# Cross-attention units of two heads and half the tokens, and three reordered steps, in a two-layer decoder trunk

## The reference, cut to what matters

```
for layer in 0, 1:
    h = RMSNorm(x);  p = h @ W_in                        # 768 columns for the mixer, 256 for the memory queries
    mix = mLSTM(p)            (layer 0, 4 heads of 192)
          DiffAttention(p)    (layer 1, 6 heads of 128)
    # memory cross-attention, 4 heads of 64, into 256 memory tokens
    q = RMSNorm(xq); k = RMSNorm(kv[:256]); v = kv[256:]
    s = q k^T / 8            per head: 512 x 256
    xo = softmax(s) v        per head: 512 x 64
    x = x + concat(mix, xo) @ W_out
    x = x + SwiGLU(RMSNorm(x))
```

## Time and profile before

| | |
|---|---|
| median of 3 runs | 1282.05 us (1280.47 to 1282.13) |
| the profiled execution | 1281.97 us |
| its span, first to last instruction | 1280.1 us, mean granted clock 0.997 |
| PE busy | 1259.7 us (98%) |
| POOL busy | 857.0 us (67%) |
| DVE busy | 538.2 us (42%) |
| ACT busy | 334.2 us (26%) |

### The profile page before, as it was taken

How to read it: one execution, slowest core, us unless ns; L and a number is a source line. 1 busy time by engine, 2 the same in 40 slices (tenths; PEclk the granted TensorE clock), 3 DMA queues, 4 the chain that set the end, 5 groups by cost and what they waited for, 6 DMA issues and landing times.

```text
span 1280.1 us, 15882 instructions
## 1 busy us (share of the span) xinstructions
PE 1259.7 (98%) x5762; PEld 1005.5 (79%) x5762; DVE 538.2 (42%) x798; ACT 334.2 (26%) x663; POOL 857.0 (67%) x1032
## 2 busy tenths in 40 slices
PE   7999999989999999999999999999999999999999
PEld 6888777668888888888878777777788888888887
DVE  6954334555333232213264777774733213321321
ACT  6423344622220011101122455553322001100110
POOL 7897332268777777777786444454677777777775
PEclk9999999999999999999999999999999999999999
DMA  7233111013222222322233222221222222232223
GB/s 258 95 129 116 50 34 50 33 54 103 98 99 99 99 86 96 99 98 99 78 119 115 66 67 66 62 75 61 74 92 98 99 98 97 90 98 94 98 78 103
DMA packets 34482, 115.92 MB, mean 91 GB/s; under 512 B 4349, under 2 KB 4862, under 8 KB 34302
## 3 DMA queue, kind: packets, MB, share of 16 engines
q1 hardware_dynamic: 32688, 111.16, 25.9%
q10 hardware_dynamic: 1742, 4.10, 1.2%
HBM read 110.00 MB, written 2.10 MB: 88 GB/s over the span
## 4 chain that ended last, share of the span: by engine, by line
PE 93%; DVE 3%; POOL 1%; issue 1%; ACT 1%; ACTq 0%; DMA 0%; SPq 0%; POOLq 0%
PE PS L1490 91%; POOL w_lo L543 1%; PE PS L1878 1%; DVE nmB L1397 1%; DVE acc L1028 1%; DVE xT L1286 0%; ACT tmp L596 0%; ACTq L847 0%; PE PS L1726 0%; DMA w_raw<-in_wt_dram 0%; PE PS L1904 0%; DVE PS L1395 0%; POOL w_hi L538 0%; PE PS L1689 0%; DVE tmp L1249 0%
## 5 line engine op out<-in xcount | busy, mean ns | idle before, releaser
L543 POOL TENSOR_TENSOR w_lo<-w_raw,w_hi 128x256 fp32r<-128x256 f32 x804 | 631.5, 816 | 17.1
L538 POOL TENSOR_SCALAR w_hi<-w_raw 128x1024 fp32r<-128x1024 f32 (+2 forms) x205 | 214.4, 1046 | 392.3 <-PE PS L1490 391.6
L1490 PE MATMUL PS<-Hh,w_hi 128*128 128x512 f32 x1072 | 432.2, 403 | 9.3 <-POOL w_lo L519 6.8
L1490 PE MATMUL PS<-Hh,w_lo 128*128 128x512 f32 x1072 | 419.0, 391 | 0.0
L1490 PE MATMUL PS<-Hl,w_hi 128*128 128x512 f32 x1072 | 418.7, 391 | 0.0
L1490 PEld LDWEIGHTS PS<-Hh,w_hi 128*128 128x128 f32 x1072 | 201.8, 188 | 67.1 <-issue 26.9
L1490 PEld LDWEIGHTS PS<-Hh,w_lo 128*128 128x128 f32 x1072 | 201.7, 188 | 43.0
L1490 PEld LDWEIGHTS PS<-Hl,w_hi 128*128 128x128 f32 x1072 | 202.1, 189 | 38.1 <-issue 1.0
L1490 PE MATMUL PS<-Ah,w_hi 128*128 128x512 f32 (+1 forms) x544 | 209.5, 385 | 0.8 <-POOL w_lo L543 0.7
L1490 PE MATMUL PS<-Al,w_hi 128*128 128x512 f32 (+1 forms) x544 | 205.4, 378 | 0.0
L1490 PE MATMUL PS<-Ah,w_lo 128*128 128x512 f32 (+1 forms) x544 | 205.3, 377 | 0.0
(11 more groups left out here) (247 smaller groups left out, 1000.6 us busy)
## 6 DMA issues: line engine op xcount, KB each, us to landing
w_raw<-in_wt_dram SPq DMA_DIRECT2D x181, 512.0 KB, 3.2
w_raw<-in_wt_dram SPq DMA_DIRECT2D x16, 384.0 KB, 3.0
w_raw<-in_wt_dram SPq DMA_DIRECT2D x8, 448.0 KB, 3.1
QKR<-QKP ACTq DMA_DIRECT2D x24, 128.0 KB, 4.3
xT<-in_x_t_dram SPq DMA_DIRECT2D x8, 256.0 KB, 5.8
out_dram<-xT SPq DMA_DIRECT2D x8, 256.0 KB, 2.0
mT<-in_mem_t_dram SPq DMA_DIRECT2D x1, 1024.0 KB, 9.2
cn<-in_constants_dram ACTq DMA_DIRECT2D x1, 580.5 KB, 6.0
```

Source lines behind the costliest of these rows:

```text
L538: nc.gpsimd.tensor_scalar(w_hi[:, sl, 0:nk], w_raw[:, raw, 0:nk], 0.0, 1.0, ALU.add, ALU.mult).then_inc(w_round, 1)
L543: lo = nc.gpsimd.tensor_tensor(w_lo[:, sl, w], w_raw[:, raw, w], w_hi[:, sl, w].bitcast(F32), ALU.subtract)
L1490: return nc.tensor.matmul(out_, a, b, start=start, stop=stop)
```

## The change

Four things.
1. In both layers a unit x now is **both heads of a pair (x // 2) and half the tokens (x % 2)**. The scores of a token tile are two adjacent products, head 0 on rows 0 to 63 and head 1 on rows 64 to 127, to different banks; the value product is, for each half of the memory tokens, two adjacent products with 64-column weights, head 0 to PSUM partitions 0 to 63 and head 1 to 64 to 127, of 256 moving columns each. The indices of scales and the tiles of `m_hi`, `m_lo` (now 128 x 256 instead of 64 x 512) follow. `c_pv` waits once, ahead of its loop.
2. Head 0: PE waits for 24 projection tiles, not 26; on ACT `cross_std(0)` comes before `head_num(0)`.
3. Last head, DVE: `m_p(3)` comes before `fill_out(7)` and `head_out(3)`.
4. Layer 0's output tile 0 is closed before tile 2 is opened, then tile 2 is opened, then 1 and 2 are closed.

```
 m_s(x), c_s(x):
-                r = 64 * (x % 2)
-                for t in range(NT):
-                    last = mm(PS[:, M_BANK[t // 2], (t % 2) * MEM:(t % 2 + 1) * MEM], xqA[r:r + 64, x // 2, t * P:(t + 1) * P],
-                              xk[r:r + 64, 0, x // 2])
-                    if t % 2:
-                        last.then_inc(ms_done, 1)
+                for i in range(2):
+                    t = 2 * (x % 2) + i
+                    for hd in range(2):
+                        r = 64 * hd
+                        last = mm(PS[:, M_BANK[hd], i * MEM:(i + 1) * MEM], xqA[r:r + 64, x // 2, t * P:(t + 1) * P],
+                                  xk[r:r + 64, 0, x // 2])
+                        if i:
+                            last.then_inc(ms_done, 1)
 m_pv(x), c_pv(x):
-                    last = mm(PS[r:r + 64, M_BANK[0]], xv[:, 0, mt, x * 64:(x + 1) * 64], M_PT[mt], start=mt == 0, stop=mt == 1)
+                    for hd in range(2):
+                        h = 2 * (x // 2) + hd
+                        last = mm(PS[64 * hd:64 * hd + 64, M_BANK[0], 0:MEM], xv[:, 0, mt, h * 64:(h + 1) * 64],
+                                  M_PT[mt][:, hd * MEM:(hd + 1) * MEM], start=mt == 0, stop=mt == 1)
 m_hi(x), and likewise m_lo, c_hi, c_lo:
-                nc.scalar.activation(Ah[r:r + 64, MC + x // 2], PS[r:r + 64, M_BANK[0]], ACT.Copy).then_inc(mo_hi, 1)
+                nc.scalar.activation(Ah[:, MC + x // 2, q], PS[:, M_BANK[0], 0:MEM], ACT.Copy).then_inc(mo_hi, 1)
 ACT, heads:
+                if h == 0:
+                    cross_std(0)
                 head_num(h)
                 if h == 0:
                     v_out(4)
-                    cross_std(0)
 DVE, heads:
                 m_max(h)
                 if h == MH - 1:
+                    m_p(h)
                     fill_out(2 * h + 1)
                 head_out(h)
...
-            m_p(MH - 1)
             mixer_out(DONE_MC, MC)
 PE, head_scores(0):
-                    pe.wait_ge(dense_free, T_HEAD)
+                    pe.wait_ge(dense_free, T_HEAD - 2)
 PE, output tiles of layer 0:
             out_blocks(1, (0, 1, 2, 3, 6), after=lambda i: m_pv(MH - 1) if i == 2 else None)
+            out_blocks(0, (4, 5, 7))
             out_blocks(2, (0, 1, 2, 3, 6))
-            for j in range(3):
-                out_blocks(j, (4, 5, 7))
+            out_blocks(1, (4, 5, 7))
+            out_blocks(2, (4, 5, 7))
```

More of the change, by code:

```diff
@@ L768, in m_exp @@
                     j = 4 * x + t
-                    nc.scalar.activation(M_P[t], PS[:, M_BANK[t // 2], (t % 2) * MEM:(t % 2 + 1) * MEM], ACT.Exp,
-                                         scale=rqA[:, x // 2, t, x % 2:x % 2 + 1], bias=nmA[:, j:j + 1],
+                    hd, q = t // 2, 2 * (x % 2) + t % 2
+                    nc.scalar.activation(M_P[t], PS[:, M_BANK[hd], (t % 2) * MEM:(t % 2 + 1) * MEM], ACT.Exp,
+                                         scale=rqA[:, x // 2, q, hd:hd + 1], bias=nmA[:, j:j + 1],
                                          accum_out=rsA[:, j:j + 1]).then_inc(ms_exp, 1)
@@ L780, in m_hi @@
             def m_hi(x):
-                r = 64 * (x % 2)
+                q = slice(MEM * (x % 2), MEM * (x % 2 + 1))
                 act.wait_ge(mo_done, x + 1)
-                nc.scalar.activation(Ah[r:r + 64, MC + x // 2], PS[r:r + 64, M_BANK[0]], ACT.Copy).then_inc(mo_hi, 1)
+                nc.scalar.activation(Ah[:, MC + x // 2, q], PS[:, M_BANK[0], 0:MEM], ACT.Copy).then_inc(mo_hi, 1)
             cross_sq(0, 0)
@@ L915, in c_exp @@
                     j = 4 * x + t
-                    nc.scalar.activation(C_P[t], PS[:, C_BANK[t // 2], (t % 2) * MEM:(t % 2 + 1) * MEM], ACT.Exp,
-                                         scale=rqB[:, x // 2, t, x % 2:x % 2 + 1], bias=nmX[:, j:j + 1],
+                    hd, q = t // 2, 2 * (x % 2) + t % 2
+                    nc.scalar.activation(C_P[t], PS[:, C_BANK[hd], (t % 2) * MEM:(t % 2 + 1) * MEM], ACT.Exp,
+                                         scale=rqB[:, x // 2, q, hd:hd + 1], bias=nmX[:, j:j + 1],
                                          accum_out=rsX[:, j:j + 1]).then_inc(cs_exp, 1)
@@ L933, in c_hi @@
             def c_hi(x):
-                r = 64 * (x % 2)
+                q = slice(MEM * (x % 2), MEM * (x % 2 + 1))
                 act.wait_ge(co_done, x + 1)
-                nc.scalar.activation(Ah[r:r + 64, MC + x // 2], PS[r:r + 64, C_BANK[1]], ACT.Copy).then_inc(co_hi, 1)
+                nc.scalar.activation(Ah[:, MC + x // 2, q], PS[:, C_BANK[1], 0:MEM], ACT.Copy).then_inc(co_hi, 1)
             b_sq(0)
@@ L1240, in m_max @@
                                                  ALU.max, negate=True))
-                    nc.vector.tensor_tensor(o, o, rqA[:, x // 2, 2 * b:2 * b + 2, x % 2], ALU.mult).then_inc(ms_max, 1)
+                    q = 2 * (x % 2)
+                    nc.vector.tensor_tensor(o, o, rqA[:, x // 2, q:q + 2, b], ALU.mult).then_inc(ms_max, 1)
             def m_p(x):
@@ L1251, in m_lo @@
             def m_lo(x):
-                r = 64 * (x % 2)
+                q = slice(MEM * (x % 2), MEM * (x % 2 + 1))
                 dve.wait_ge(mo_hi, x + 1)
-                nc.vector.tensor_tensor(Al[r:r + 64, MC + x // 2], PS[r:r + 64, M_BANK[0]],
-                                        Ah[r:r + 64, MC + x // 2].bitcast(F32), ALU.subtract).then_inc(mo_ready, 1)
+                nc.vector.tensor_tensor(Al[:, MC + x // 2, q], PS[:, M_BANK[0], 0:MEM],
+                                        Ah[:, MC + x // 2, q].bitcast(F32), ALU.subtract).then_inc(mo_ready, 1)
             for h in range(MH):
@@ L1424, in c_max @@
                                                  ALU.max, negate=True))
-                    nc.vector.tensor_tensor(o, o, rqB[:, x // 2, 2 * b:2 * b + 2, x % 2], ALU.mult).then_inc(cs_max, 1)
+                    q = 2 * (x % 2)
+                    nc.vector.tensor_tensor(o, o, rqB[:, x // 2, q:q + 2, b], ALU.mult).then_inc(cs_max, 1)
             def c_rec(x):
@@ L1431, in c_lo @@
             def c_lo(x):
-                r = 64 * (x % 2)
+                q = slice(MEM * (x % 2), MEM * (x % 2 + 1))
                 dve.wait_ge(co_hi, x + 1)
-                nc.vector.tensor_tensor(Al[r:r + 64, MC + x // 2], PS[r:r + 64, C_BANK[1]],
-                                        Ah[r:r + 64, MC + x // 2].bitcast(F32), ALU.subtract).then_inc(co_ready, 1)
+                nc.vector.tensor_tensor(Al[:, MC + x // 2, q], PS[:, C_BANK[1], 0:MEM],
+                                        Ah[:, MC + x // 2, q].bitcast(F32), ALU.subtract).then_inc(co_ready, 1)
             for c in range(MC):
@@ L1889, in c_s @@
             def c_s(x):
-                r = 64 * (x % 2)
                 pe.wait_ge(bv_ready, x + 1)
                 pe.wait_ge(bat_ready, 4 * x + 4)
[L1894 to L1898, removed]
+                for i in range(2):
+                    t = 2 * (x % 2) + i
+                    for hd in range(2):
+                        r = 64 * hd
+                        last = mm(PS[:, C_BANK[hd], i * MEM:(i + 1) * MEM], xqB[r:r + 64, x // 2, t * P:(t + 1) * P],
+                                  xk[r:r + 64, 1, x // 2])
+                        if i:
+                            last.then_inc(cs_done, 1)
             def c_t(x):
@@ L1907, in c_pv @@
             def c_pv(x):
-                r = 64 * (x % 2)
+                pe.wait_ge(ct_ready, 2 * x + 2)
                 for mt in range(MT_TILES):
-                    pe.wait_ge(ct_ready, 2 * x + 2)
-                    last = mm(PS[r:r + 64, C_BANK[1]], xv[:, 1, mt, x * 64:(x + 1) * 64], C_PT[mt], start=mt == 0, stop=mt == 1)
+                    for hd in range(2):
+                        h = 2 * (x // 2) + hd
+                        last = mm(PS[64 * hd:64 * hd + 64, C_BANK[1], 0:MEM], xv[:, 1, mt, h * 64:(h + 1) * 64],
+                                  C_PT[mt][:, hd * MEM:(hd + 1) * MEM], start=mt == 0, stop=mt == 1)
                 last.then_inc(co_done, 1)
```

## The result

The changed kernel takes **1259.36 us** (median of 4 runs, 1259.07 to 1259.66); the kernel before 1281.26 us (4 runs, 1278.89 to 1282.13). The ratio is 0.983, 95% interval 0.9815 to 0.9849: 1.7% faster. Forecast were 1259.6 us and a range of 1257.5 to 1267. The profiled execution took 1259.66 us, span 1257.9, against 1281.97 and 1280.1.

A forecast was written before the change was run, and what follows sets the result against it. PE, busy for 98% of the span, was taken to bound the kernel. Savings of 6.8 + 6.8 + 2.64 + 0.95 + 2.74 + 1.78 + 0.72 = 22.4 us from 1281.97 gave 1259.6 us, range 1257.5 to 1267.

The forecast's parts named there:

- 1a: Scores, 8 units: the two heads run side by side on row halves, 0.85 us saved each, 6.8 us.
- 1b: Values, 8 units: the two heads run side by side on column halves, 0.85 us saved each, 6.8 us.
- The row pair of the earlier trace: Layer 1's two products on rows 0 to 63 and 64 to 127, 1.06 us, taken as the units' price.
- Part 2: Head 0: gap and half clock gone, 2.64 us; `cross_std(0)` hidden in ACT's idle time, 0.95 us.
- Part 3: Last head: wait before the transposes gone, 2.74 us after 0.1 lost; half clock behind it gone, 1.78 us.
- Part 4: Layer 0's output tiles: closing tile 0 early removes the wait before tile 3, 0.72 us.
- A cost that I put at nothing: Layer 1 cross-attention units: smaller costs come out at nothing, with 1.2 us of slack between `c_lo` and `b_t(c, 1)`.
- The 1.70 us of half clock at head 0: Scores of head 0: 6.28 us against head 2's 4.58; the clock was expected to stay up without the gap.
- B: Values: column halves don't run side by side, so they gain nothing; 1266.4 us, chance 0.17.
- C: Last head: the new order brings its own wait, up to 1.5 us; 1261 to 1263 us, chance 0.13.
- D: Scores and values: pairs overlap only when alone, so neither set of four gains; 1273.2 us, chance 0.04.
- E: Scores and values: each change between row or column halves drains the array; slower, 1293.7 us, chance 0.03.

The follow-up runs named there:

- wait_26_tiles: The changed kernel with head 0's wait for all 26 projection tiles put back on PE; 1260.93 us.
- std_late: The changed kernel with `cross_std(0)` put back behind `head_num(0)` and `v_out(4)` on ACT; 1260.05 us.
- tiles_old_order: The changed kernel with layer 0's first three output tiles all opened, then closed in turn, as before; 1260.36 us.
- values_one_half: The changed kernel with value products ordered head 0, 0, 1, 1 and head 1 also on PSUM partitions 0 to 63; 1265.78 us.
- half_products: The changed kernel with score and value products ordered by head, each cut into two of 128 moving columns; 1267.61 us.
- values_by_head: The changed kernel with a unit's four value products ordered head 0, 0, 1, 1 in both layers; 1259.49 us.
- m_p_late: The changed kernel with `m_p(3)` put back behind `fill_out(7)` and `head_out(3)`; 1263.69 us.
- units_only: The kernel before with only the new units (two heads, half the tokens), old waits and orders kept; 1267.83 us.

## Why the prediction was right
**Sum and steps.** 1281.97 - 1259.66 = 22.3 us in the profiled executions, 22.4 forecast; 21.9 us between the medians. The two traces can be laid side by side, dense product against dense product, to see where the gain arises. **Parts 1a and 1b**: 8 x 0.86 = 6.9 and 8 x 0.85 = 6.8 us measured from the starts of all units, 6.8 and 6.8 forecast. The row pair of the earlier trace rows was the right price for both, for the scores to the hundredth. **Part 2**: 2.6 us at head 0 (2.64 forecast) and 0.99 us at the root's wait (0.95); both waits returned in wait_26_tiles and std_late. **Part 3**: 4.7 us for the wait and the half clock behind it, 4.52 forecast. The 0.1 us that I counted as lost was not: `m_p(3)` took 3.2 us in all instead of 3.4, and was 0.3 us early. **Part 4**: 0.96 us, 0.72 forecast, and it came back when the order did. The terms of parts 3 and 4 are small in part because I took the brackets for the cost of the stalls (see tiles_old_order). The start of the profiled execution was 0.5 us slower than before's (the four-row product at 144.39 instead of 143.9), which hides half a microsecond of the gain in the spans.

**A cost that I put at nothing.** Behind the last cross-attention unit of layer 1 the changed kernel gives 0.27 us back. I had read 1.2 us of slack between `c_lo` and `b_t(c, 1)` from one unit. At the last one there was less: `c_lo` ended at 847.77 and the three transposes followed at 848.15. First the kernel before, then the changed one:
```profile
847.08 0.69 DVE L1434 TENSOR_TENSOR Al<-PS,Ah 64x512 fp32r<-64x512 f32 x1
848.15 0.49 PE L1878 MATMUL PS<-cn,PB 128*128 128x128 f32 x3
```
```profile
825.29 0.42 DVE L1439 TENSOR_TENSOR Al<-PS,Ah 128x256 fp32r<-128x256 f32 x1
825.37 0.40 PE L1495 MATMUL PS<-Hh,w_lo 128*128 128x512 f32 x1
825.86 0.52 PE L1888 MATMUL PS<-cn,PB 128*128 128x128 f32 x3
```
Now `c_lo` ends at 825.71, and PE starts the transposes 0.49 us after the dense product before them, where the pace is 0.23. That the wait is for `c_lo` is inferred from the source and these times. In values_one_half, where PE comes later, the 0.27 us is not there; it is about half of the difference between the 6.8 us forecast for that kernel and the 6.3 measured.

**Where it was right by luck.** The 1.70 us of half clock at head 0, and the 1.78 us behind the last transposes, were counted as certain. The same 0.94 us gap brought the first in the profile of the kernel before, and not in two profiles with the gap; the four runs of wait_26_tiles split evenly. The second stood in all three profiles with the long wait, and seems to be missing in 3 of 31 runs of the kernel before. The time forecast for the changed kernel does not hang on this: both stretches were in the 1281.97 us that I started from, and both came off. The gain does: it is about 21 us against the 16 runs of the kernel before that read as one stretch, and under 20 against the 3 that read as none. That part of the forecast rested on one execution.

**The rivals.** B (column halves in turn) is excluded by 1.01 us a unit, and values_one_half shows what it would have been: 1265.8 us, forecast 1266.4. With it falls the strict reading of the rule in the Trainium skill ("TensorE: Matmul & The Clock Gate", Part 3, The mechanism) that a weight load overlaps a running matmul only with another row group: here both heads' weights use all rows. The rows at hand spoke against it already: PE was busy for 98% of the span and its weight loads for 79% of the same span, most of them for dense products on all rows. C did not happen: margins of 0.3 and 2.0 us, where I had 0.2 and 1.4. D and E, lone pairs and drains, are excluded by the units' times.

**The step with a wrong reason.** I gave the alternation of the heads in the list as what lets them run together. It is not needed for four products; the half of the array is. With eight records of one half in a row it cost 0.49 to 0.55 us a group (half_products), so some alternation is needed there.

## What to carry to other kernels
Where two small products use different rows of the array, or different columns, put them near one another: here a group of such products took 1.06 us instead of 1.92, and 1.01 instead of 1.86, at plain float32. Order them so that no more than about four records of one half stand ahead of the other's first (four cost 7 ns, eight cost half a microsecond a group); and choose the unit of work so that both halves are busy, here two heads and half the tokens, at the same count of other engines' instructions. A stall on a busy TensorE can cost more than itself, since the clock can fall behind it: 1.8 us more behind 2.84 us of waiting here. Whether it falls differs from one execution to the next, so read the mean granted clock of several runs before counting on it. And read the slack at every repetition of a step, not at one.

## What was not expected of the hardware
- The first records of two halves start 7 ns apart when they are two places apart in the list, 13 ns when they are four. With eight, the second half starts 0.49 to 0.55 us later, at head 0's fifth record. The Trainium skill ("TensorE: Matmul & The Clock Gate", Part 3, The mechanism) calls matmuls strictly first in, first out in start and end. Here, in values_by_head, the fifth and sixth records of the list (head 1 on `tmp`) start before the third (head 0 on `QK`), so the measurement decides against that for the starts.
- The pair on column halves costs as little as the pair on row halves (1.01 and 1.06 us a unit).
- The granted clock fell to 0.52 behind a gap of 0.94 us in one profile and stayed at 1.00 behind the same gap in two others. Behind a wait of 2.8 to 2.9 us it fell in all three profiles that have one (the kernel before, m_p_late, units_only), but three runs of the kernel before and one of m_p_late have a mean clock of 1.000 and times some 1.5 us lower, which suggests that it does not always.
